# Expert pairs chosen by sorted row count, with uneven halves, and three early weight pieces held until the first gather lands

## The reference, cut to what matters

```python
g_logits = hf @ w_rg + b_rg                      # 4 groups, the best one is taken
e_sel = take_along_axis(hf @ w_re + b_re, g_idx) # its 8 experts, the best two
weights = pg_top * pe_top / sum(pe_top)
for e in range(32):
    act = silu(hf @ w_gate[e]) * (hf @ w_up[e])
    y = y + combine[:, e:e + 1] * (act @ w_down[e])
return x + gate2 * y
```

## Time and profile before

| | us |
|---|---|
| median of 3 runs | 1676.64 (1675.55 to 1677.65) |
| the profiled execution | 1675.31 |
| its span | 1673.4 |
| PE busy | 1571.5 (94%) |
| dense part, to about | 1383 |
| expert part, gate and up of the first tile start at | 1406.66 |

### The profile page before, as it was taken

How to read it: one execution, slowest core, us unless ns; L and a number is a source line. 1 busy time by engine, 2 the same in 40 slices (tenths; PEclk the granted TensorE clock), 3 DMA queues, 4 the chain that set the end, 5 groups by cost and what they waited for, 6 DMA issues and landing times.

```text
span 1673.4 us, 19707 instructions
## 1 busy us (share of the span) xinstructions
PE 1571.5 (94%) x8009; PEld 1183.4 (71%) x8009; DVE 825.1 (49%) x1442; ACT 543.1 (32%) x881; POOL 84.3 (5%) x106
## 2 busy tenths in 40 slices
PE   7999999999999999999999899999999996888875
PEld 7987777777787788888887688787678883333322
DVE  6546334355355776666323884437663736222211
ACT  5334444354433322222113433342354323111110
POOL 5000000000000000000000010000000001121110
PEclk9999999999999999999999999999999996989998
DMA  5334212122233455565222232221214467999995
GB/s 164 116 101 128 76 51 76 51 76 76 69 95 114 151 183 190 186 221 176 101 101 89 60 103 87 89 66 62 76 51 151 159 231 303 382 414 403 402 407 188
DMA packets 147070, 260.41 MB, mean 156 GB/s; under 512 B 16568, under 2 KB 121316, under 8 KB 133664
## 3 DMA queue, kind: packets, MB, share of 16 engines
q1 hardware_dynamic: 138544, 241.41, 41.1%
q0 software_dynamic: 8432, 17.70, 3.6%
HBM read 253.79 MB, written 15.25 MB: 161 GB/s over the span
## 4 chain that ended last, share of the span: by engine, by line
PE 83%; DVE 7%; issue 4%; ACT 3%; DMA 2%; POOL 0%; POOLq 0%; DVEq 0%; ACTq 0%
PE psum L2498 20%; PE psum L2499 20%; PE psum L2500 20%; PE psum L3079 7%; PE psum L3096 4%; PE psum L2809 1%; PE psum L2798 1%; PE psum L2781 1%; PE psum L3057 1%; DVE cst L2012 1%; DVE WL L1560 1%; DMA Xg<-h_rows,tok 1%; PE psum L2703 1%; ACT Sb L1114 1%; DMA h_rows<-h2t 1%
## 5 line engine op out<-in xcount | busy, mean ns | idle before, releaser
L1560 DVE TENSOR_TENSOR WL<-raw,WH 128x2048 fp32r<-128x2048 f32 (+1 forms) x100 | 226.6, 2266 | 177.1 <-ACT WH L1029 176.8
L2498 PE MATMUL psum<-AHs,WH 128*128 128x512 f32 x744 | 305.9, 411 | 7.5 <-DVE WL L1560 4.6
L2500 PE MATMUL psum<-AHs,WL 128*128 128x512 f32 x744 | 292.6, 393 | 0.0
L2499 PE MATMUL psum<-ALs,WH 128*128 128x512 f32 x744 | 292.1, 393 | 0.0
L1029 ACT ACTIVATE WH<-raw 128x2048 fp32r<-128x2048 f32 (+1 forms) x100 | 189.0, 1890 | 129.1 <-PE psum L2500 97.7
L2498 PEld LDWEIGHTS psum<-AHs,WH 128*128 128x128 f32 x744 | 141.4, 190 | 44.3 <-DVE ALs L1748 5.8
L2498 PE MATMUL psum<-AH,WH 128*128 128x512 f32 (+1 forms) x464 | 169.2, 365 | 0.0
L2499 PE MATMUL psum<-AL,WH 128*128 128x512 f32 (+1 forms) x464 | 164.0, 353 | 0.0
L2499 PEld LDWEIGHTS psum<-ALs,WH 128*128 128x128 f32 x744 | 141.6, 190 | 30.9 <-issue 3.1
L2500 PE MATMUL psum<-AH,WL 128*128 128x512 f32 (+1 forms) x464 | 163.2, 352 | 0.0
L2500 PEld LDWEIGHTS psum<-AHs,WL 128*128 128x128 f32 x744 | 140.9, 189 | 30.7
(11 more groups left out here) (561 smaller groups left out, 2277.4 us busy)
## 6 DMA issues: line engine op xcount, KB each, us to landing
raw<-w_in SPq DMA_DIRECT2D x45, 1024.0 KB, 5.2
WE<-w_gate SPq DMA_DIRECT2D x34, 1024.0 KB, 19.3
WE<-w_up SPq DMA_DIRECT2D x34, 1024.0 KB, 23.1
WE<-w_down SPq DMA_DIRECT2D x34, 1024.0 KB, 19.0
araw<-w_ada SPq DMA_DIRECT2D x24, 1024.0 KB, 5.6
raw<-w_ffn_in SPq DMA_DIRECT2D x22, 1024.0 KB, 7.9
raw<-w_ffn_out SPq DMA_DIRECT2D x11, 1024.0 KB, 4.9
raw<-w_out SPq DMA_DIRECT2D x8, 1024.0 KB, 5.4
```

The source lines that it names most:

```text
L1560: V.tensor_tensor(WL[:, n, 0:w], raw[:, n, 0:w], WH[:, fed[0] % HL, 0:w].bitcast(F32), ALU.subtract).then_inc(S_("lo_ready"), 1)
L2498: MM(dst, lh, rh, start=first, stop=False)
L2499: MM(dst, lh, rl, start=False, stop=False)
L2500: return MM(dst, ll, rh, start=False, stop=last)
```

## The change

1. **16 tiles that always run, not 17.** `BASE` is 16 and there is no tile for overflow. The branch for further blocks now has 15 single tiles and is taken at more than 0 blocks, not at more than 2.
2. **Pairs by sorted row count.** In each half of the experts, 13 (`SORTED`) are put in order of their row count on DVE (`sorted_places`); the first half's experts go to tiles 3 to 15 from the most rows to the fewest, the second half's from the fewest to the most. SP reads the experts of a tile from the table `order`. Tiles 0 to 2 (`HELD`) have fixed experts: 13 to 15 with 29 to 31.
3. **Uneven halves.** In tiles 3 and 4 the first expert has 96 rows and the second 32; in tiles 14 and 15 it is 32 and 96. A share of 96 rows is multiplied in two matmuls, of 64 and of 32 columns, so each group of two matmuls becomes one of three (`parts_of`).
4. **Routing numbers later.** Before the first gather DVE finds the tokens of tiles 0 to 2 alone. The others' numbers are worked out behind the first copies of tile 0 (`widths`) and behind its gating (`rows_and_pairs`, `token_weights`); their tokens, the weights by row and the scaling of tile 0's result stand behind the gating of tile 1. PE's small matmuls for these (`overflow_spots`, `weights_by_row`) stand behind `gate_up(1)`. Gathers from tile 3 on use the later table.
5. **Held pieces.** Of the early weight pieces, down of tile 1's second half, gate of tile 2's first and up of its second are issued when the first gather has landed.

```diff
-BASE = NE // 2 + 1
-NPAIR = BASE + NOV - 2
-
-OVER = 3
+BASE = NE // 2
+NPAIR = BASE + NOV
+
+HELD = 3
+SORTED = NE // 2 - HELD
+WIDE = 2
...
+        def held(t, half):
+            return NE // 2 * half + SORTED + t
+
+        def parts_of(t):
+
+            if t >= BASE:
+                return [(0, CAP, 0)]
+            if HELD <= t < HELD + WIDE:
+                return [(0, 64, 0), (64, 96, 0), (96, 128, 1)]
+            if t >= BASE - WIDE:
+                return [(0, 32, 0), (32, 64, 1), (64, 128, 1)]
+            return [(0, 64, 0), (64, 128, 1)]
...
             sp.wait_ge(*when("dense_ready", len(GROUPS)))
-            load_expert(sp, 1, 1, 1)
-            load_gate(sp, 2, 0, 2, 0)
-            sp.wait_ge(*when("h2_stored", 16 * NB))
-            load_gate(sp, 2, 1, NE // 2 + 2, 1)
-            sp.wait_ge(*when("overflow_ready", 1))
...
+            load_gate_up(sp, 1, 1, held(1, 1))
+            sp.wait_ge(*when("xg_landed0", 16))
+            load_down(sp, 1, 1, held(1, 1))
+            load_gate(sp, 2, 0, held(2, 0), 0)
+            load_gate(sp, 2, 1, held(2, 1), 1)
+            sp.wait_ge(*when("order_ready", 1))
             sp.wait_ge(*when("out_set", 16 * 3))
...
+            for t in range(HELD, BASE):
+                load_pair(sp, t, [sp.value_load(order[0:1, x:x + 1], min_val=0, max_val=NE - 1)
+                                  for x in (t - HELD, SORTED + t - HELD)])
...
             def rows_of_pair(t):
-                return (tok if t < BASE and t != OVER else tok2)[:, t:t + 1]
+                return (tok if t < HELD else tok2)[:, t:t + 1]
...
-            pool.wait_ge(*when("over_tokens", 1))
             for t in range(BASE):
+                if t + 2 == HELD:
+                    pool.wait_ge(*when("over_tokens", 1))
...
                 xt_copy(t0)
                 if t0 == 0:
-                    overflow_numbers()
-                    overflow_tokens()
-                    token_weights()
+                    widths()
                 for t in range(t0, t1):
                     gated(t)
+                    if t == 1:
+                        overflow_tokens()
+                        weights_by_row()
+                        y_scaled(0)
+                        overflow_numbers()
                     if t + 1 < t1:
                         xt_copy(t + 1)
                     if t == 0:
-                        weights_by_row()
+                        rows_and_pairs()
+                        token_weights()
+                        continue
                     y_scaled(t)
...
                 for k in range(KC):
-                    for half in halves(t):
-
-                        rows = slice(CAP * half, CAP * half + CAP)
-                        ins = MM(bank(3)[rows], XT[:, t % 2, P * k + CAP * half:P * k + CAP * half + CAP],
+                    for lo, hi, half in parts_of(t):
+
+                        ins = MM(bank(3)[lo:hi], XT[:, t % 2, P * k + lo:P * k + hi],
                                  GU[gate_up_slot(t, half)].rearrange("p (g k n) -> p k g n", g=2, k=KC)[:, k],
                                  start=k == 0, stop=k == KC - 1)
```

More of the change, by code:

```diff
@@ L969, in scatter @@
                     pool.wait_ge(*when("out_set", 16 * 3))
[L970 to L978, removed]
+                pool.indirect_dma_start(out=out[0], out_offset=bass.IndirectOffsetOnAxis(ap=rows_of_pair(t), axis=0),
+                                        in_=Yt[:, t % 2, :], in_offset=None, bounds_check=S - 1, oob_is_err=False,
+                                        compute_op=ALU.add).then_inc(S_(f"y_stored{t % 2}"), 16)
             def out_columns(c0, c1):
@@ new lines, in widths @@
+            def widths():
+                link(V.tensor_scalar(wider, places[:, 1, :], HELD - 0.5, None, ALU.is_ge))
+                link(V.scalar_tensor_tensor(wider, places[:, 1, :], HELD + WIDE - 0.5, wider, ALU.is_ge, ALU.subtract))
+                link(V.scalar_tensor_tensor(wider, places[:, 1, :], BASE - WIDE - 0.5, wider, ALU.is_ge, ALU.add))
+                for side in range(2):
+                    half = slice(NE // 2 * side, NE // 2 * side + NE // 2)
+                    link(V.tensor_scalar(cap[:, half], wider[:, half], 64.0 * side - 32.0, float(CAP), ALU.mult, ALU.add))
+                link(V.tensor_tensor(cnt, cnt, cap, ALU.subtract))
+                full_blocks(over, cnt, thr[:, 0, :], steps7[0])
+                link(V.memset(base_, 1.0))
+                link(V.tensor_tensor_scan(incl, base_, over, 0.0, ALU.mult, ALU.add))
+                link(V.tensor_tensor(base_, incl, over, ALU.subtract))
+                for n, x in ((2, places[:, 0, :]), (3, places[:, 1, :]), (4, base_), (7, cap)):
+                    chosen(by_tile[n], x.unsqueeze(1).unsqueeze(1), prod[1])
@@ L2407, in overflow_tokens @@
                 dve.wait_ge(*when("spots_used", 1))
[L2408 to L2412 removed]
+                token_of(tok2, 6, NPAIR).then_inc(S_("over_tokens"), 1)
             def token_weights():
@@ L3026, in _ @@
             for n in range(2 * NB):
[L3027 removed]
+                ins = MM(bank(5, 2 * HELD), inrow[0][:, n, :], inpair[0][:, n].rearrange("p c n -> p (c n)"), start=n == 0,
                          stop=n == 2 * NB - 1)
@@ L3092, in down @@
                     for j in range(2):
-                        for half in halves(t):
-                            rows = slice(CAP * half, CAP * half + CAP)
+                        for lo, hi, half in parts_of(t):
                             o = 2 * DE * KC + D * j + 512 * n
-                            ins = MM(bank(4 + n)[rows], AT[:, t % 2, P * j + CAP * half:P * j + CAP * half + CAP],
+                            ins = MM(bank(4 + n)[lo:hi], AT[:, t % 2, P * j + lo:P * j + hi],
                                      WE[(2 * t + half) % SLOTS][:, o:o + 512], start=j == 0, stop=j == 1)
```

154 lines of the change are left out of this document (84 added, 70 removed).

## The result

| | before | after |
|---|---|---|
| median, us | 1677.14 (4 runs, 1675.55 to 1679.15) | 1704.19 (4 runs, 1701.89 to 1705.94) |
| profiled execution | 1675.31 | 1703.56 |
| its span | 1673.4 | 1701.8 |

The ratio is 1.0161, with an interval of 1.0146 to 1.0177: 27 us slower. The direction of the forecast was right, its size wasn't: it said 1692, and the measured median lies above its range, which ended at 1702.

The account below looks back on a forecast made before the run. The DMA bound the kernel before; PE would be the new bound. Tile 3 from 1449.5, plus 78.9 (tiles 3, 4, 14), 123.3 (5 to 13), 24.8 and 12.6: span 1689.1, plus 3.2: 1692 us, range 1681 to 1702.

Parts of the forecast that it names:

- The gather of tile 3: POOL issues it behind scatter 0, now 8 us later; lands about when PE asks, costing 1.0 us (0 to 2).
- wait for gather 3, to tile 3's start: Tile 3's gate and up start at 1450.4 - 2.9 + 1.0 + 1.0 = 1449.5.
- tiles 3 and 4: Uneven tiles on PE, each put at 13.7 + 12.6 = 26.3 us; 52.6 for both.
- from tile 15's start: The end: 24.8 us remaining behind the last tile's start, plus 12.6 for its mixed widths; 37.4.
- What bounds the kernel before: Expert part bound by the DMA, 17.1 us a tile against PE's 13.7, by 20 us.
- One tile less, 15.1 us: 34 pieces each of gate, up and down become 32; 15.1 us of DMA time go if the DMA stays the bound.
- The start, 2.9: First gather goes out 1.9 us earlier and takes 1.0 less; gain 2.9 us (0 to 4.3), moving the DMA's stream too.
- The numbers moved: Routing work behind tiles 0 and 1: DVE's mostly covered, PE's small groups 1.0 us new, gather 3 another 1.0.
- Uneven halves: Tiles 3, 4, 14, 15: mixed widths don't overlap, a group takes 1.90 us instead of 0.86, 12.6 us a tile.
- rival (a): Uneven tiles' matmuls: widths mix freely, the DMA stays the bound, kernel faster at 1658.6 us; chance 0.14.
- Tiles 5 to 13 at PE's pace: These tiles take 13.7 us each, 123.3 in all, without waiting for weights; the DMA stays ahead of PE.

Follow-up runs that it names:

- both edits: Changed kernel, 64- and 32-column matmuls kept, experts of odd tiles from 3 on in exchanged halves, gather of tile 3 ahead of scatter of tile 0: 1695.42 us, ratio 1.0116.

## Why the prediction was right in sign and wrong in size

Two steps of the sum failed. The gather of tile 3 was sized at 1.0 us and cost 5.8 (DVE's numbers and PE's small groups took 0.6, not 1.0, so together 6.4 stand against 2.0), and tiles 5 to 13 were put at PE's pace without a wait for weights, where they took 6.8 us more. What decided the sign, the cost of the mixed widths, was right to 1 us a tile. The range was made of that cost and of the start alone, so neither step that failed had a share in it.

The sum had the span at 1689.1; it is 1701.8, so 12.7 us are missing. By its own steps, from the chain of the kernel after:

| step | forecast | measured | miss |
|---|---|---|---|
| tile 1's gate and up | 1420.1 | 1418.52 | -1.6 |
| wait for gather 3, to tile 3's start | 1449.5 | 1452.34 | +4.4 |
| tiles 3 and 4 | 52.6 | 53.90 | +1.3 |
| tiles 5 to 13 | 123.3 | 130.08 | +6.8 |
| tile 14 | 26.3 | 27.15 | +0.9 |
| from tile 15's start | 37.4 | 38.33 | +0.9 |

**What bounds the kernel before**: right. The DMA was the bound. Whoever takes the change and only evens the widths out (four of 32 columns) finds the stretch from tile 0's to the last tile's start 232.2 us long, where before had 1648.64 - 1406.66 = 242.0.

**One tile less, 15.1 us**: the size was right only with balanced halves. With fixed sides 9.8 of it arrived; with the halves exchanged 1634.24 - 1404.85 = 229.4, so 12.6, and with the gather early as well 1630.3 - 1402.2 = 228.1, so 13.9. Each is one profiled run, the last one the fastest of its four.

**The start, 2.9**: right where it arises, and not found again at the end. Tile 1 did start 4.5 us earlier in the profiled run, but 1.0 of that lies ahead of all that was changed. From the first copy to `h2t` on ACT to tile 0's gate and up it took 1402.69 - 1382.20 = 20.5 us, where before had 1406.66 - 1383.19 = 23.5, so 3.0 less. Alone, the held pieces gave 0.06% (-0.04 to 0.16%), 1 us, at the end, and with equal widths they gave nothing that can be told.

**The numbers moved**: DVE's part held: from tile 1's start to tile 2's it took 14.3 us, 0.6 more than 13.7. The gather of tile 3 failed. It was sized at 1.0 (0 to 2) as landing "about when PE asks". It was issued at 1431.40 behind scatter 0, ran 11.53 us beside the scatter and full DMA engines, and PE, done at about 1439.6, waited 3.3 us; then down ran on a slow clock, 6.11 for 3.65:

```profile
1439.60:1446.20 6.60, 1.44 (x12) 1.21 (x11) 1.79 (x5) 2.16 (x6) 2.62 (x2) 0.86 1.02 423
1446.20:1452.30 6.10, 6.08 (x17) 2.10 (x18) 0.00 (x0) 0.00 (x0) 0.00 (x0) 0.59 1.02 395
```

3.3 + 2.5 = 5.8 us of this trace. Taking the wait away gave less in the end, 1.7 to 4.0 us, since the DMA then holds PE up later (waits of 1.76 and 2.94 us ahead of tiles 13 and 14 in that run). The step gave the gather no duration; "about when PE asks" fits the 4.90 us of a moment with the DMA half idle, while in the kernel before the gather behind the overflow tile's scatters already took 9.61:

```profile
1477.35 9.61 DMA Xg<-h_rows,tok
```

It also left out what a wait does to the clock.

**Uneven halves**: right in mechanism, short by 1 us a tile in size, and it decides the case. The forecast group was 1.90 us; PE's timeline of tile 3 (start, us, what; a row joins several records):

```profile
1452.58 1.15 PE L3133 MATMUL psum<-WE,XT 128*64 128x512 f32 x3
1453.10 1.05 PE L3133 MATMUL psum<-WE,XT 128*32 128x512 f32 x4
1453.56 1.17 PE L3133 MATMUL psum<-WE,XT 128*32 128x512 f32 x3
1454.09 1.07 PE L3133 MATMUL psum<-WE,XT 128*64 128x512 f32 x2
1454.57 1.15 PE L3133 MATMUL psum<-WE,XT 128*64 128x512 f32 x3
```

A change takes 0.52 (1452.58 to 1453.10) and 0.53 (1453.56 to 1454.09), which bears out what was read from the earlier trace rows (0.53 there, which the forecast wrote as 0.52). The step between two passes of equal width was put at 0.43, but behind a change it is 0.46 (1453.10 to 1453.56) and 0.48 (1454.09 to 1454.57). The group is 1.985 us; times 12 groups that is 1 us more a tile, and the uneven tile costs 13.3, not 12.6. The rule that the forecast set against its rival (a) held: of these matmuls, of 64 and 32 columns, only equal widths overlap. The Trainium skill, page TensorE: Matmul & The Clock Gate, section Part 3: Packing small matmuls, says that matmuls in distinct column groups run concurrently. By that alone it would have been the rival's 1658.6, and 1704 was measured; with equal widths the runs agree with the page, four of 32 columns in 6.87 us.

**"Tiles 5 to 13 at PE's pace"** failed, and it is the largest miss. The step let the DMA arrive at tile 14 with 5 us to spare, at "about 1620", which its own numbers don't give: tile 14 of the kernel before began, with a short wait, at 1614.81, and 1614.81 - 2.9 + 12 = 1623.9. The DMA then paused 17.3 us, not 12, and at tiles 12 and 13 its later half ran 12.4 to 12.8 us behind, where an even share would have put both halves some 6 behind the earlier one. For tile 13 that makes 1597.45 - 4.5 + 17.3 + 6.3 = 1616.6, an estimate from the earlier trace rows and these figures; PE was ready at 1616.13 and started at 1619.58, so 3 us of the lateness stay open. So PE waited 3.44 us at tile 13, and gate and up behind the wait took 9.90 for 6.87:

```profile
1606.00:1616.00 10.00, 8.25 (x42) 3.59 (x38) 1.79 (x5) 2.17 (x6) 1.37 (x2) 1.00 1.02 400
1616.00:1619.50 3.50, 0.13 (x2) 0.00 (x0) 1.41 (x2) 0.00 (x0) 0.98 (x1) 0.85 1.01 425
1619.50:1629.50 10.00, 9.92 (x33) 3.25 (x33) 0.00 (x0) 0.00 (x0) 1.63 (x2) 0.71 1.02 398
```

3.44 + 3.03 = 6.5 of the 6.8. With both edits made, the median is 1695.4, and the forecast's sum gives 1692 + 4 = 1696 when only the group is corrected. That it fits to 1 us is in part luck: in that run's trace tiles 5 to 13 still took 3.0 us more than the 123.3 of the sum.

**What stays open**: which waits of PE are followed by the slow clock. Behind 3.44 us it fell here (mean 0.71), behind 3.25 in the kernel before it didn't (7.09 for gate and up). The length of the wait alone doesn't decide it: with four of 32 columns and exchanged halves, a wait of 2.62 us was followed by 8.78 for gate and up, and in the kernel before with one side fixed one of 3.27 by 7.09. And the four runs with exchanged halves and uneven widths spread over 9.5 us, so the gain of that edit alone is rough; with the gather the spread is 3.7. And no run mixes other widths than 64 and 32.

## What to carry to other kernels

Before columns of the array are shared out unevenly, cut all parts of a group to one width: here matmuls of 64 and 32 columns didn't overlap though their columns are disjoint, and four of 32 columns cost the same as two of 64. Where rows are gathered or scattered and some are empty, count the full rows in partitions 0 to 63 and 64 to 127 along the run; a mean DMA share of 1.02 hides that one half is late, and a plateau at half the rate near the end, seen in steps of 2 us, gives it away. And read what a rewrite drops, not only what it adds: one exchanged pair of arguments was worth 5.7 us in the kernel before. All of the change's idea with equal widths and exchanged halves gives 1659.9, 1.0% faster than before.

## What the runs showed of the hardware

- The halves of the DMA engines drifted 15 us apart under full load (share 1.02), with 250 full rows more in rows 0 to 63 than in rows 64 to 127, and 3 us with the sides exchanged; a weight piece is complete with the later half.
- Between matmuls of 64 and of 32 columns (float32, 512 elements streamed) the step was 0.52 to 0.53 us in place of 0.43, and the next step of equal width was longer too, 0.46 for 32 columns and 0.48 for 64.
- A gather took 3.9 us with the DMA engines at a share of 0.36, and 11.5 us beside a scatter with the engines full.
